# A state-space scan whose group norm is finished one turn later, with its squares summed on VectorE

## The reference

```python
y = jnp.concatenate(ys, axis=1) + xs.astype(f32) * D_skip.astype(f32)[:, None]
u = y.reshape(b, L, SSD_INNER) * jax.nn.silu(z.astype(f32))
ug = u.reshape(b, L, SSD_GROUPS, SSD_INNER // SSD_GROUPS)
ug = ug * lax.rsqrt(jnp.mean(ug * ug, axis=-1, keepdims=True) + EPS)
u = (ug.reshape(b, L, SSD_INNER) * norm_w.astype(f32)).astype(h.dtype)
y_ssd = u @ w_ssd_out
```

## Time and profile before

| | us |
|---|---|
| Median of 3 runs (1414.89 to 1416.55) | 1415.66 |
| Profiled execution, its own time | 1419.62 |
| Its span in the profile | 1417.8 |
| TensorE busy | 1328.1 (94%) |
| VectorE busy | 555.9 (39%) |
| GpSimd busy | 477.4 (34%) |
| ScalarE busy | 377.6 (27%) |

### The profile page before, as it was taken

One profiled execution on the slowest core, in us unless ns is written; L12 is line 12 of the kernel. 1 busy time (PEld: TensorE's weight loads), 2 busy tenths in 40 slices (PEclk: granted clock), 3 DMA queues, 4 the chain that ended last, 5 costly groups with the idle time before them and its releaser, 6 DMA issues.

```text
span 1417.8 us, 23366 instructions
## 1 busy us (share of the span) xinstructions
PE 1328.1 (94%) x9207; PEld 1029.9 (73%) x9207; DVE 555.9 (39%) x804; ACT 377.6 (27%) x574; POOL 477.4 (34%) x379
## 2 busy tenths in 40 slices
PE   4999999999989999998989999999987999999992
PEld 4999999999759876976887699996465444444440
DVE  5444531016556754865675560011143221121122
ACT  4211224433333423433342352110012111111112
POOL 5444432334332532544263253431001222222211
PEclk8999999999989998999999899999985999999997
DMA  5223222225106203510631223245921899999964
GB/s 145 75 74 89 74 60 74 75 78 146 31 9 177 74 15 96 133 44 0 170 88 44 67 62 88 75 135 162 399 97 38 314 355 361 361 371 374 383 217 145
DMA packets 180169, 204.73 MB, mean 144 GB/s; under 512 B 13945, under 2 KB 155385, under 8 KB 171858
## 3 DMA queue, kind: packets, MB, share of 16 engines
q1 hardware_dynamic: 167972, 187.97, 40.1%
q0 software_dynamic: 8192, 9.83, 3.0%
q10 hardware_dynamic: 3942, 6.06, 1.2%
HBM read 189.45 MB, written 29.72 MB: 155 GB/s over the span
## 4 chain that ended last, share of the span: by engine, by line
PE 76%; DVE 12%; issue 4%; ACT 3%; DMA 3%; SPq 1%; DVEq 1%; ACTq 0%; POOLq 0%
PE acc L590 36%; PE pT L964 8%; PE acc L825 5%; PE pS L977 4%; PE acc L1001 4%; DVE area L1181 4%; PE pS L1011 2%; PE pY L753 2%; PE pS L697 2%; DMA ring<-in_w_in 1%; PE acc L929 1%; PE acc L719 1%; DVE big L1252 1%; PE pS L759 1%; PE pY L936 1%
## 5 line engine op out<-in xcount | busy, mean ns | idle before, releaser
L590 PE MATMUL acc<-h_parts,ring_parts 128*128 128x328 f32 (+1 forms) x3840 | 553.0, 306 | 12.2 <-DVE h_parts L1079 6.9
L590 PEld LDWEIGHTS acc<-h_parts,ring_parts 128*128 128x128 f32 x3840 | 539.2, 192 | 29.0 <-issue 28.2
L1763 POOL TENSOR_TENSOR ring_parts<-ring,ring_parts 128x1024 fp32r<-128x1024 f32 x104 | 264.5, 2544 | 421.7 <-ACT ring_parts L1496 421.7
L1496 ACT ACTIVATE ring_parts<-ring 128x1024 fp32r<-128x1024 f32 x104 | 110.0, 1058 | 372.4 <-PE acc L590 354.9
L964 PE MATMUL pT<-area,big 128*64 128x512 f32 x384 | 115.3, 606 | 0.2 <-ACT big L1691 0.2
L590 PE MATMUL acc<-u_parts,ring_parts 128*128 128x264 f32 (+1 forms) x640 | 109.4, 299 | 0.0
L590 PEld LDWEIGHTS acc<-u_parts,ring_parts 128*128 128x128 f32 x640 | 96.4, 188 | 0.0
L1181 DVE SCALAR_TENSOR_TENSOR area<-area,xvec 128x616 f32<-128x616 f32 x72 | 90.1, 1252 | 10.5 <-DVE area L1179 0.6
L964 PEld LDWEIGHTS pT<-area,big 128*64 128x64 f32 x384 | 35.2, 139 | 78.2 <-issue 78.2
L590 PE MATMUL acc<-area_parts,ring_parts 128*128 128x264 f32 (+1 forms) x512 | 91.1, 299 | 0.0
L590 PEld LDWEIGHTS acc<-area_parts,ring_parts 128*128 128x128 f32 x512 | 78.4, 188 | 0.0
(11 more groups left out here) (332 smaller groups left out, 1721.3 us busy)
## 6 DMA issues: line engine op xcount, KB each, us to landing
ring<-in_w_in SPq DMA_DIRECT2D x80, 512.0 KB, 3.9
area<-in_w_gate SPq DMA_DIRECT2D x24, 1024.0 KB
area<-in_w_up SPq DMA_DIRECT2D x24, 1024.0 KB
area<-in_w_down SPq DMA_DIRECT2D x24, 1024.0 KB
area<-in_state_ssm SPq DMA_DIRECT2D x16, 512.0 KB, 6.7
out<-area SPq DMA_DIRECT2D x16, 512.0 KB, 5.3
ring<-in_w_ssd_out SPq DMA_DIRECT2D x16, 512.0 KB, 4.1
ring<-in_w_gate SPq DMA_DIRECT2D x8, 1024.0 KB
```

The costliest lines, as they stand in the source:

```text
L590: m = nc.tensor.matmul(acc[a][:, h, 0:n], w[s][:, k, :], x[:, k, h * HALF:h * HALF + n], start=first and k == 0 and w is w_hi and x is hi, ...
L1496: a_.activation(w_hi[b % 2], w_raw[b % 2], ACT.Copy).then_inc(hi_done, 1)
L1763: gp.tensor_tensor(w_lo[b % 2], w_raw[b % 2], w_hi[b % 2].bitcast(F32), ALU.subtract).then_inc(lo_done, 1)
```

## The change

The squares of the four feature tiles are summed on VectorE in two instructions (in place, in `sq`), and TensorE sums only one tile over the partitions: one matmul per half of the tokens instead of four. VectorE signals the sum with a second increment of `s_sq`.

The norm's last steps leave the end of the turn. The reciprocal and the multiplications of the first two tiles of group g come after tile 0's features in turn g + 1, those of the other two tiles after tile 1's. The first turn is written out without them, and the last group's norm follows the loop. The norm's weight gets a buffer of its own (`dgn`), since `dg` is loaded for the next group by then. The root lies in the last tile of `sz`; so ScalarE waits for `s_un` before it evicts block 9 into that tile, and the casts of groups 2 and 3, which lie over it, wait until the last group's norm is done.

```diff
--- before.py
+++ after.py
@@ -89,6 +89,7 @@
         e_acum, dte, dec = (sb(n, [P, TILES, HEADS]) for n in ("e_acum", "dte", "dec"))
         sdec = sb("sdec", [R4, HEADS])
         dg = sb("dg", [P, GK, 2])
+        dgn = sb("dgn", [P, GK, 1])
 
 
         BIG, RING, AREA = 40 * T, 6 * BLK, 19852
@@ -157,7 +158,7 @@
         rbuf, o = carve(o, [2, 4 * P])
         bmask, _ = carve(o - 8 * P, [NSEQ, NST])
         wts, o = carve(o, [2, 4 * P])
-        rms, _ = carve(o, [T])
+        rms = sz[:, GK - 1, :]
         ytok, o = carve(o, [GW])
         cbm, o = carve(o, [P])
         hs, o = carve(o, [GK, NSEQ, NST])
@@ -792,12 +793,10 @@
                 pe.wait_ge(s_hs, g * 4 + 4)
 
                 pe.wait_ge(s_so, g + 1)
-                pe.wait_ge(s_sq, g + 1)
+                pe.wait_ge(s_sq, 2 * g + 2)
                 for h, pb in ((0, pT), (1, pS)):
                     n = HALF if h == 0 else T - HALF
-                    for k in range(GK):
-                        m = nc.tensor.matmul(pb[:, 0:n], ones[:, :], sq[:, k, h * HALF:h * HALF + n],
-                                             start=k == 0, stop=k == GK - 1)
+                    m = nc.tensor.matmul(pb[:, 0:n], ones[:, :], sq[:, 0, h * HALF:h * HALF + n], start=True, stop=True)
                 m.then_inc(p_gn, 1)
 
             for n in range(1, 4):
@@ -1165,8 +1164,22 @@
             start += link.count[0]
             with dve.Fori(2, 8) as f:
                 o1_turn(f)
-            with dve.Fori(0, GROUPS) as g:
-                link = chain(dve, dve_chain, start, g, 25)
+            def norm_tiles(g, ks):
+                for k in ks:
+                    u_k = uT[:, bass.ds(g * GK + k, 1), :].rearrange("p a b -> p (a b)")
+                    x = v.scalar_tensor_tensor(u_k, u_k, dgn[:, k, :], rms, ALU.mult, ALU.mult)
+                return x
+
+            def norm_root(g, link):
+                link(v.tensor_copy(dgn[:, :, :], dnv[:, bass.ds(g * GK, GK), 1:2]))
+                dve.wait_ge(s_rm, g + 2)
+                link(v.reciprocal(rms, rms))
+
+            def norm_end(g):
+                norm_tiles(g, (2, 3)).then_inc(s_un, 1)
+                dve.wait_ge(s_un, g + 2)
+
+            def scan_turn(g, link, first):
                 link(v.tensor_copy(dg[:, :, :], dnv[:, bass.ds(g * GK, GK), :]))
                 v.memset(st, 0.0).then_inc(s_st, 1)
                 for c in range(6):
@@ -1240,20 +1253,34 @@
                         x = v.scalar_tensor_tensor(u_k, xT[:, k, tok(i)], dg[:, k, 0:1], pY[:, k * P:k * P + r],
                                                    ALU.mult, ALU.add)
                     x.then_inc(s_u, 1)
+                    if i == 0 and not first:
+                        norm_root(g - 1, link)
+                        norm_tiles(g - 1, (0, 1))
+                    if i == 1 and not first:
+                        norm_end(g - 1)
 
                 dve.wait_ge(s_sz, g + 1)
                 dve.wait_ge(s_u, g * 5 + 6)
                 u_g = uT[:, bass.ds(g * GK, GK), :]
                 v.tensor_tensor(u_g, u_g, sz, ALU.mult).then_inc(s_uz, 1)
-                dve.wait_ge(s_rm, g + 2)
-                link(v.reciprocal(rms, rms))
-                for k in range(GK):
-                    u_k = uT[:, bass.ds(g * GK + k, 1), :].rearrange("p a b -> p (a b)")
-                    x = v.scalar_tensor_tensor(u_k, u_k, dg[:, k, 1:2], rms, ALU.mult, ALU.mult)
-                x.then_inc(s_un, 1)
-                dve.wait_ge(s_un, g + 1)
-                assert link.count[0] == 25, link.count
-            start += GROUPS * 25
+                dve.wait_ge(s_sq, 2 * g + 1)
+                link(v.tensor_tensor(sq[:, 0:2, :], sq[:, 0:2, :], sq[:, 2:4, :], ALU.add))
+                v.tensor_tensor(sq[:, 0, :], sq[:, 0, :], sq[:, 1, :], ALU.add).then_inc(s_sq, 1)
+
+            dve.sem_inc(s_un, 1)
+            link = chain(dve, dve_chain, start)
+            scan_turn(0, link, True)
+            start += link.count[0]
+            with dve.Fori(1, GROUPS) as g:
+                link = chain(dve, dve_chain, start - 27, g, 27)
+                scan_turn(g, link, False)
+                assert link.count[0] == 27, link.count
+            start += (GROUPS - 1) * 27
+            link = chain(dve, dve_chain, start)
+            norm_root(GROUPS - 1, link)
+            norm_tiles(GROUPS - 1, (0, 1))
+            norm_end(GROUPS - 1)
+            start += link.count[0]
 
             for c in range(1, 4):
                 u_c = uT[:, 4 * c:4 * c + 4, :]
@@ -1577,6 +1604,8 @@
                     use, _, a, ause = g_block(g, 6 + k)
                     act.wait_ge(w_done, use + 2)
                     split_hi(g_block(g, 6 + k), k)
+                    if k == GK - 1:
+                        act.wait_ge(s_un, g + 1)
                     a0, a1 = acc_parts(acc[a])
                     d0, d1 = halves(sz[:, k, :])
                     a_.activation(d0, a0, ACT.Copy)
@@ -1644,7 +1673,7 @@
                     gate_of(where, gate_at(n), 9 if n < 4 else n + 6)
 
             for c in range(4):
-                act.wait_ge(s_un, c + 1)
+                act.wait_ge(s_un, c + 2 if c < 2 else GROUPS + 1)
                 a_.activation(uT_hi[:, 4 * c:4 * c + 4, :], uT[:, 4 * c:4 * c + 4, :], ACT.Copy).then_inc(u_hi, 1)
                 if c == 1:
                     gate_of(gate_block(0), gate_at(0), 9)
```

## The result

The change makes the kernel slower: 1421.34 us against 1414.53 for the kernel before on the same chips (medians of 12 runs each), a ratio of 1.0048 [1.0038, 1.0058], or 6.8 us. The forecast was 1416.3 and its likeliest case "no change"; the time lies inside the range, at its upper end, near rival (b), which had 1420.6. That it lies inside owes something to chance: the difference of 6.8 us is more than the 5.8 by which the range's upper end stands above the 1415.66 it was reckoned from, and the time fits because the kernel before had 1414.53 over twelve executions. Two far outlying executions among those of the experiments, one of the shorter insertion (3967.6 us) and one of the norm in four pieces (1669.3 us), are left out of all medians. The profiled execution took 1424.2 us, its span 1422.5, so 4.7 us more than the span of before.

A forecast was written before the change was run, and what follows sets the result against it. TensorE carries 76% of the chain, so only its waits or removed work count. Won 14.0 us (boundaries, end, waits), lost 14.6 (11.7 + 0.3 + 2.6): net +0.6 on 1415.66 gives 1416.3 us, range 1411.0 to 1421.5.

The forecast's parts named there:

- no change: Whole kernel: time between 1412.8 and 1418.5 us, within about 0.2% of the kernel before; chance 0.50.
- rival (b): Tile 1: clock falls at the new stall every turn at full price, insertion at its upper end; +4.9, 1420.6 us; chance 0.19.
- Part 3: Between tiles 0 and 1: reciprocal and two multiplications insert 6.4 us against 2.5 slack; stall 3.9 a turn, 11.7 in all.
- Part 6: Behind tile 1's stall: lower clock slows the following products by 0.9 us a turn, 2.6 in all (0 to 4.5).
- Parts 1 and 2: Turn boundaries: fewer norm matmuls win 2.2, 2.2 and 1.2 us; norm leaving the head removes 6.9 us of TensorE's waits.
- Part 5: Behind the last turn: earlier norm matmuls bring the root 1.5 us earlier; GpSimd's split just in time; 1.5 us won.
- Part 4: Between tiles 1 and 2: the other two multiplications nearly fit the 2.5 us slack; 0.1 us lost a turn, 0.3 in all.
- (a): Tile 1: the clock holds and GpSimd's work is not met; -4.1 us, 1411.6; chance 0.14 for beyond -2.8.
- (c): Head of turn: GpSimd or raw weights late, or VectorE not limiting; 4 of 6.9 us stay; 1420.3; chance 0.11.
- (d): Tiles: the norm is fully hidden and all 14 us are kept, 1401.7; chance 0.06, including a good part of it.
- Both are one event: Tile 1: argument that a longer stall from the insertion makes the lower clock surer, so the two losses come together.

The follow-up runs named there:

- the shorter insertion: Changed kernel with half the reciprocal and the small copy moved before tile 0's sum with TensorE's product: 1412.55 us, 0.9957 against the kernel before.
- the norm in four pieces: Changed kernel with the norm cut up and laid where VectorE waits in tiles 0 to 2, no insertion in the way: 1403.9 us, 0.9902; again 1399.83, 0.9892.
- the stall with TensorE kept busy: Changed kernel with four unread matmuls filling TensorE's wait in tile 1 of turns 1 to 3: 1418.06 us, 1.0029; again 1415.51, 1.0006.
- the version that only defers: Changed kernel with the 16 norm matmuls and without VectorE's sums, the norm still deferred: 1428.14 us, 1.0073 against the kernel before.

## Where the prediction was right, and where it was wrong

It forecast +0.6 us as the likeliest and 6.8 came. The mechanism, a stall of TensorE in tile 1 that eats what the heads win, is right. By stretch the 7.0 us between +0.6 and the profile's +7.6 are the stall and the clock behind it (4.2), the heads (3.1), the end (1.5) and 0.1 in tile 2, less 1.9 ahead of the norm, where the clock of block 10 differs.

**The place and size of the stall (Part 3): right.** Forecast 3.9 a turn and 11.7 in all, came 3.9 and 11.8. The insertion was put at 6.4 us and measured 6.57: the reciprocal 3.85 as in the earlier trace rows, the multiplications 2.37 for the pair, between their medians (1.6 to 1.7) and the worst of the earlier trace rows. Both ends are shown: 1.58 us without GpSimd beside them (the shorter insertion), 2.37 with its decay product, which itself grew from 1.04 us to 1.59. That agrees with the rule of the Trainium skill, page "GPSIMD Engine Reference", section "8. Key points", that the prediction weighed.

**The clock (Part 6): the term that was mis-sized.** The prediction took 0.9 us a turn, 2.6 in all, with 1.5 a turn as its bound. The step that failed is the count of what is lost: "the products behind it (L703's, and the half block of 4.18 us) lose 0.7 to 1.5 us a turn". The traces have 3.0, 1.8 and 1.9, 6.7 us in all (the 18.5 of the table less 11.8 of waits), and the stall with TensorE kept busy shows 6.0 less in the trace and 7.0 less in the time. The place was right: from the start of L704 to L754's start it is 7.34, 6.12 and 6.19 us in turns 1 to 3, where it was 4.47 before, and the tile's own product behind it takes its 1.89 us as before. The size was not: in turn 1 the clock was low through L704 and into most of the half block, 2.9 us lost, and even the shorter stretches of turns 2 and 3 cost 1.7 there. The clock fell in every turn. A wait of 1.0 us (the shorter insertion) left the clock full three times of three; a wait of 3.9 us never did in the traces looked at. The Trainium skill, page "TensorE: Matmul & The Clock Gate", section "Why this matters for your kernels", advises against such gaps; these runs agree, with about 2 us for each.

**The heads of the turns (Parts 1 and 2): right in what goes, wrong in what is late next.** The sums took 1.39 + 0.78 us where 2.4 were put, the block starts 3.15 us behind the Square's end where 3.3 were forecast, and both old waits went. The prediction looked for the next limit at the weights of that block and found 0.7 us to spare, which held. It didn't look at the block's accumulator, which ScalarE frees only at 570.75, though it had read in the earlier trace rows that this eviction stands behind the root at 570.68. TensorE now asks at 569.77. Three times 1.0 us: 15.3 forecast less 3.1 is the 12.2 that came. Ahead of the norm the profile has +0.9 where +2.8 were forecast, but that says little of the sums: block 10 itself changed by -1.1, +0.2 and +1.0 us with the clock, and the stretch by -1.4, -0.5 and +2.7.

**The end (Part 5): wrong.** Of the 1.5 us 0.1 is left at the first matmul with u, and nothing behind the projection. Counted from the last state transposes, the root came 0.7 us earlier and the gate blocks went on 0.7 us earlier (24.6 us behind the transposes before, 23.9 after); TensorE's wait for the eviction grew from 0.72 to 1.55. Then GpSimd's split was 0.5 us late: "that just holds" did not. The four multiplications took 8.44 us beside GpSimd, against 5.22 in the earlier trace rows.

**Tile 2 (Part 4): right,** 0.13 us a turn for the forecast 0.1.

**The rivals.** (a) is out: the clock fell and GpSimd was met, in every turn. (b) came nearest. That its time is within a microsecond is luck, since its difference was +4.9 and +6.8 came, and it got there by other terms: it put the insertion at its upper end and 1.5 a turn for the clock, and what came was the likely insertion and 2.2 for the clock. "Both are one event" was the right reading, and 0.19 was too low a chance for it: its condition, more than 4.7 us lost in tile 1, was met in each turn, with 7.0, 5.7 and 5.8. (c) came in part, 3.1 of its 4 us, by a wait that it didn't name. (d), all 14.0 kept, is near what the version without insertion has: -14.4, -14.2. The agreement is in part luck: in its first trace the heads give 11.3 us (12.5 forecast), the end 0.8 (1.5), and 4.1 come from tile 4, where nothing was forecast: 3.3 because the clock stayed full in all four turns, 0.8 in turn 0. So most of the 14 us counted as won were there. The reason against (d), that L703 waits for the mask product and the order of the program keeps it behind the norm, held for this placement and not for the idea.

## What to carry to other kernels

Work moved off one engine's critical stretch has to be put behind the last result of that engine that TensorE is waiting for, and in pieces no longer than the slack in front of the next: the same 9 us of norm (6.57 and 2.37) made the kernel 6.8 us slower in two pieces, and 14 faster when laid between products that TensorE did not need yet (some 3 of the 14 are the clock in tile 4). A stall of TensorE that lowers its clock costs more than its length, here 3.9 us and about 2 us more. When a wait is taken out of the way of a block, go through everything that the next block needs, its accumulator as well as its weights.

## What the runs showed of the hardware

- The granted clock fell at every stall of 3.9 us that was looked at (nine: three turns each in two traces of the change and one of the version that only defers), and at the three of 10.9 us. The loss (1.8 to 3.0 us in the change) varied with the turn for the same stall. Waits of 1.0 us and of 1.8 us (L698 in tile 0) left it full.
- A reciprocal of 128x592 takes 3.85 us, of 128x296 1.99: nearly five times a multiplication with two tensors of that size (0.79).
- A pair of 128x592 multiplications took 1.58 us alone and 2.37 beside a GpSimd product of 128x512, which took 1.59 instead of 1.04: both engines paid.
- The clock in tile 4, where TensorE is busy most of the time with small matmuls, fell in some turns and not in others, and changed between versions that don't touch it. It moved 1.6 us a turn each way, once 3.2, as much as the smaller edits here are worth; its cause is open.
